# Recurrence heads taken in pairs, scores as 32x32 blocks, and three more query blocks split in high and low parts

## The reference, cut to what matters

```python
q, f_pre, i_v, g, a, a_gate = split(x @ w_in)          # 4 heads of 128 each; a, a_gate: 512 channels
f = lb + (1 - lb) * sigmoid(f_pre)
k = (1 - lb) * sigmoid(-f_pre)
b = cumsum(log(f)) within chunks of 32 tokens          # 8 chunks
q_t = q * exp(b);  k_t = k * exp(-b);  k_end = k * exp(b_last - b)
scores = where(causal, q_t @ k_t.T, 0)                 # 32 x 32 in each chunk and head
o_intra = scores @ v
d_state = k_end.T @ v                                  # 128 x 128 in each chunk and head
state[n + 1] = exp(b_last[n]) * state[n] + d_state[n]
o = o_intra + q_t @ state[n]                           # then rms norm per head, times silu(g)
u = causal_conv31(a * sigmoid(a_gate)) + cv_b          # 31 taps, then layer norm and silu
y = concat(o, u) @ w_out
```

## Time and profile before

| what | before |
|---|---|
| median of 3 runs | 1241.21 us (1241.1 to 1242.23) |
| profiled execution | 1241.21 us |
| its span | 1239.4 us |
| PE, DVE, ACT busy | 1231.4, 801.4, 672.7 us |
| POOL busy | 30.8 us |

### The profile page before, as it was taken

How to read it: one execution, slowest core, us unless ns; L and a number is a source line. 1 busy time by engine, 2 the same in 40 slices (tenths; PEclk the granted TensorE clock), 3 DMA queues, 4 the chain that set the end, 5 groups by cost and what they waited for, 6 DMA issues and landing times. The chain is left out here.

```text
span 1239.4 us, 16273 instructions
## 1 busy us (share of the span) xinstructions
PE 1231.4 (99%) x6332; PEld 1048.4 (85%) x6332; DVE 801.4 (65%) x1185; ACT 672.7 (54%) x1034; POOL 30.8 (2%) x36
## 2 busy tenths in 40 slices
PE   9999999999999999999999999999999999999997
PEld 8888888888888888899988888888888888888886
DVE  5655556878767555568999765755557674755455
ACT  7555546668574444465776745544445754744441
POOL 0000000010000000000001000000001000000000
PEclk9999999999999999999999999999999999999999
DMA  9755556452355555554354632755554443565540
GB/s 368 276 185 178 190 180 201 156 194 85 109 181 187 187 187 187 187 159 174 114 182 158 215 121 104 271 187 188 188 188 166 171 153 119 204 221 189 187 167 34
DMA packets 60891, 219.96 MB, mean 177 GB/s; under 512 B 6672, under 2 KB 8208, under 8 KB 60176
## 3 DMA queue, kind: packets, MB, share of 16 engines
q1 hardware_dynamic: 60528, 218.55, 51.8%
q10 hardware_dynamic: 288, 0.39, 0.1%
HBM read 217.86 MB, written 1.05 MB: 177 GB/s over the span
## 5 line engine op out<-in xcount | busy, mean ns | idle before, releaser
L1212 DVE TENSOR_TENSOR w_lo<-w_raw,w_hi 128x1024 fp32r<-128x1024 f32 x387 | 472.7, 1228 | 341.0 <-ACT w_hi L642 339.9
L642 ACT ACTIVATE w_hi<-w_raw 128x1024 fp32r<-128x1024 f32 x387 | 407.3, 1058 | 421.5 <-PE bank L2049 400.3
L2047 PE MATMUL bank<-w_hi,x_hl 128*128 128x512 f32 (+2 forms) x912 | 357.9, 392 | 0.1
L2049 PE MATMUL bank<-w_hi,x_hl 128*128 128x512 f32 (+2 forms) x912 | 353.1, 387 | 0.0
L2048 PE MATMUL bank<-w_lo,x_hl 128*128 128x512 f32 (+2 forms) x912 | 352.8, 387 | 0.0
L2049 PEld LDWEIGHTS bank<-w_hi,x_hl 128*128 128x128 f32 x912 | 171.2, 188 | 34.9
L2047 PEld LDWEIGHTS bank<-w_hi,x_hl 128*128 128x128 f32 x912 | 171.4, 188 | 34.3 <-issue 0.6
L2048 PEld LDWEIGHTS bank<-w_lo,x_hl 128*128 128x128 f32 x912 | 171.5, 188 | 32.8
L2047 PE MATMUL bank<-w_hi,h_hi 128*128 128x512 f32 (+1 forms) x364 | 141.9, 390 | 0.0
L2049 PE MATMUL bank<-w_hi,h_lo 128*128 128x512 f32 (+1 forms) x364 | 141.3, 388 | 0.0
L2048 PE MATMUL bank<-w_lo,h_hi 128*128 128x512 f32 (+1 forms) x364 | 141.2, 388 | 0.0
(11 more groups left out here) (323 smaller groups left out, 1399.6 us busy)
## 6 DMA issues: line engine op xcount, KB each, us to landing
w_raw<-weights_d SPq DMA_DIRECT2D x394, 512.0 KB, 3.3
arena<-ln_rows_d SPq DMA_DIRECT2D x3, 1024.0 KB, 5.6
arena<-weights_d SPq DMA_DIRECT2D x4, 512.0 KB, 5.0
arena<-late_d SPq DMA_DIRECT2D x1, 1056.0 KB, 8.4
arena<-first_d SPq DMA_DIRECT2D x2, 512.0 KB, 5.5
xs<-x_d SPq DMA_DIRECT2D x2, 512.0 KB, 7.2
kv_mem<-mem_d SPq DMA_DIRECT2D x1, 1024.0 KB, 12.3
out_d<-kv_mem SPq DMA_DIRECT2D x3, 256.0 KB, 2.1
```

The lines of the kernel that those rows point to most:

```text
L642: nc.scalar.activation(w_hi[:, slot(b), :], w_raw[:, b % RAW, :], ACT.Copy).then_inc(hi_ready, 1)
L1212: nc.vector.tensor_tensor(w_lo[:, slot(b), :], w_raw[:, b % RAW, :], w_hi[:, slot(b), :].bitcast(F32), ALU.subtract).then_inc(lo_ready, 1)
L2047: nc.tensor.matmul(out, wh, xh, start=start, stop=False, skip_group_check=True)
L2049: return nc.tensor.matmul(out, wl, xh, start=False, stop=stop, skip_group_check=True)
```

## The change

WHOLE loses steps 12, 13 and 14 of ab_in, so these three query blocks are split. Fewer convolution taps stand ahead of steps 10 to 12, and ACT's taps are spread anew over the steps. Scores are made as 32x32 blocks, only those on the diagonal, side by side in half a bank, and masked in one instruction; their product with v becomes eight 32x32 products a head in place of two of 128x128. The recurrence takes heads 0 and 1, then 2 and 3: changes of state of two heads lie side by side in the four banks, DVE makes the states of both in turns, and PE has the gate blocks 1 and 2 between the changes of the first pair and the wait for its states. States of heads 2 and 3 have a place of their own.

```diff
@@ -85,7 +85,7 @@
     NB += _count
-WHOLE = [FIRST["ab_in"] + n for n in (0, 1, *range(10, 15))]
+WHOLE = [FIRST["ab_in"] + n for n in (0, 1, 10, 11)]
 
@@ -137,7 +137,7 @@
 NCST = 0
-for _name, _cols in [("rows_all", 158), ("causal", P), ("rope", 4 * ROPE), ("dist", 2 * S), ("spread", 4 * P)]:
+for _name, _cols in [("rows_all", 158), ("causal", HG_CHUNK), ("rope", 4 * ROPE), ("dist", 2 * S), ("spread", 4 * P)]:
     CST[_name] = NCST
@@ -153,7 +153,7 @@
     put("rows_all", w)
-    put("causal", (p[:, None] // HG_CHUNK == p[None, :] // HG_CHUNK) & (p[:, None] <= p[None, :]))
+    put("causal", p[:, None] % HG_CHUNK <= np.arange(HG_CHUNK)[None, :])
     pos = np.arange(S, dtype=np.float32)
@@ -255,7 +255,7 @@
 
-        causal = const("causal", 0, P)
+        causal = const("causal", 0, HG_CHUNK)
 
@@ -332,12 +332,12 @@
         eb, _ = region(s0, HG_HEADS, S)
-        sc, _ = region(s0, 2, 512)
+        sc, _ = region(s0, 2 * HG_HEADS, HG_CHUNK)
         s1 = at
...
         go_on = kv_mem[:, 3, 0:4 * S].rearrange("p (a b) -> p a b", b=S)
-        ho_sq_buf, _ = region(s1, 2, HALF)
         s2 = at
+        ho_sq_buf, _ = region(s2, 2, HALF)
         hk, at = region(at, HG_HEADS, S)
@@ -352,9 +352,17 @@
         state = [xs[:, 4 * k:4 * k + 4, 1, :].rearrange("p c (n v) -> p c n v", v=P) for k in range(2)]
+        late_state, late_end = region(s0 + 2 * HG_HEADS * HG_CHUNK, 2 * (NCHUNK - 1), P)
+        assert late_end <= s2
 
         def state_of(h, n):
-            return state[h % 2][:, n // 2, n % 2, :]
+            if h < 2:
+                return state[h][:, n // 2, n % 2, :]
+            return late_state[:, (h - 2) * (NCHUNK - 1) + n - 1, :]
+
+        def change_of(h, n):
+            at = h % 2 * S + n // 4 * P
+            return PB[n % 4][:, at:at + P]
 
@@ -1051,7 +1059,7 @@
 
-            TAP_AT = {4: [(0, 0), (0, 1), (1, 0), (1, 1)], 5: [(0, 2), (1, 2)], 7: [(0, 3), (1, 3)], 8: [(2, 0), (2, 1)], 10: [(2, 2)], 11: [(2, 3)], 13: [(3, 0)], 14: [(3, 1), (3, 2), (3, 3), (4, 0)], 15: [(4, 1)], 16: [(4, 2), (4, 3)], 17: [(5, 0), (5, 1), (5, 2), (5, 3)], 18: [(6, 0), (6, 1), (6, 2), (6, 3)], 19: [(7, 0), (7, 1), (7, 2)]}
+            TAP_AT = {4: [(0, 0), (0, 1), (1, 0), (1, 1)], 5: [(0, 2), (1, 2)], 7: [(0, 3), (1, 3)], 10: [(2, 0), (2, 1)], 11: [(2, 2), (2, 3)], 13: [(3, 0)], 14: [(3, 1), (3, 2)], 15: [(3, 3)], 16: [(4, 0), (4, 1), (4, 2)], 17: [(4, 3), (5, 0), (5, 1), (5, 2)], 18: [(5, 3), (6, 0), (6, 1), (6, 2)], 19: [(6, 3), (7, 0), (7, 1)]}
             ends = flat(bsum).rearrange("p (g s) -> p g s", s=HG_CHUNK)[:, :, HG_CHUNK - 1:HG_CHUNK]
@@ -1098,28 +1106,28 @@
 
-            make_taps([(7, 3), (8, 0), (8, 1), (8, 2), (8, 3)])
-
-            for h in range(HG_HEADS):
-                if h == HG_HEADS - 2:
-                    act.wait_ge(tap_added, 8)
-                    done(FIRST["ab_g"] + 3)
+            make_taps([(7, 2), (7, 3), (8, 0), (8, 1), (8, 2), (8, 3)])
+
+            def squares(pair):
+                act.wait_ge(ho_ps, pair + 1)
+                for h in (2 * pair, 2 * pair + 1):
                     for t in range(2):
-                        nc.scalar.activation(hg[:, t, :], PB[6 + t][:, :], ACT.Silu).then_inc(g_silu, 1)
-                if h == HG_HEADS - 1:
-                    blk()
-                    blk()
-                    mem_blocks(1, 2, 3)
-                act.wait_ge(ho_ps, h + 1)
-                for t in range(2):
-                    w, k = slice(h * P, (h + 1) * P), 2 * h + t
-                    nc.scalar.activation(ho_sq_buf[:, t, w], PB[4 + t][:, w], ACT.Square, accum_out=ho_ss[:, k:k + 1]).then_inc(ho_sq, 1)
-                make_taps(([], [(9, 0), (9, 1), (9, 2), (9, 3)], [], [])[h])
-                if h == 0:
-                    act.wait_ge(ho_sq, 2)
-                    nc.scalar.activation(ho_sq_buf[:, 0, 0:1], decay[:, 0:1], ACT.Silu)
-                elif h < HG_HEADS - 1:
-                    blk()
+                        w, k = slice(h * P, (h + 1) * P), 2 * h + t
+                        nc.scalar.activation(ho_sq_buf[:, t, w], PB[4 + t][:, w], ACT.Square, accum_out=ho_ss[:, k:k + 1]).then_inc(ho_sq, 1)
+
+            blk()
+            blk()
+            nc.scalar.activation(neg_max[0][:, 0:1], decay[:, 0:1], ACT.Silu)
+            squares(0)
+            act.wait_ge(tap_added, 8)
+            done(FIRST["ab_g"] + 3)
+            for t in range(2):
+                nc.scalar.activation(hg[:, t, :], PB[6 + t][:, :], ACT.Silu).then_inc(g_silu, 1)
+            make_taps([(9, 0), (9, 1), (9, 2), (9, 3)])
+            blk()
+            squares(1)
+            blk()
+            mem_blocks(1, 2, 3)
             mem_blocks(1, 3, 5)
@@ -1888,12 +1896,11 @@
                 dve.wait_ge(hk_ready, 4)
-                for t in range(2):
-                    nc.vector.copy_predicated(sc[:, t, :].rearrange("p (h q) -> p h q", q=P), bc(causal.bitcast(I32), HG_HEADS),
-                                              PB[t][:, :].rearrange("p (h q) -> p h q", q=P)).then_inc(sc_ready, 1)
+                nc.vector.copy_predicated(sc[:, :, :], bc(causal.bitcast(I32), 2 * HG_HEADS),
+                                          half(1, 1).rearrange("p (h q) -> p h q", q=HG_CHUNK)).then_inc(sc_ready, 1)
 
             dve.wait_ge(ones_set, 5)
-            ahead = (0, 0, 2, 1, 3, 0, 0, 0, 3, 0, 10, 6, 8, 0, 1, 4, 0, 0, 0, 2)
+            ahead = (0, 0, 2, 1, 3, 0, 0, 0, 3, 0, 7, 3, 5, 0, 1, 4, 0, 0, 0, 2)
             behind_lo = (0, 0, 3, 0, 3, 0, 14, 0, 0, 0, 0, 0, 0, 0, 0, 0, 0, 0, 0, 0)
             add_ahead = {8: (0, 2), 13: (2, 3), 14: (3, 4), 18: (4, 6)}
@@ -1931,27 +1938,37 @@
             add_taps(6, 7)
-            conv_taps(3)
-
-            for h in range(HG_HEADS):
-
-                if h >= 2:
-                    dve.wait_ge(ho_ps, h - 1)
+            conv_taps(4)
+
+            def states(pair):
+                heads = (2 * pair, 2 * pair + 1)
                 dve.wait_ge(e_ready, 3)
-                dve.wait_ge(ds_ps, (NCHUNK - 1) * (h + 1))
-                mark(nc.vector.tensor_copy(state_of(h, 1), PB[0][:, 0:P]))
+                dve.wait_ge(ds_ps, (NCHUNK - 1) * (2 * pair + 2))
+                at = {}
+                for h in heads:
+                    mark(nc.vector.tensor_copy(state_of(h, 1), change_of(h, 0)))
+                    at[h] = chain[0]
                 for n in range(1, NCHUNK - 1):
-                    settle()
-                    ins = nc.vector.scalar_tensor_tensor(state_of(h, n + 1), state_of(h, n),
-                                                         decay[:, h * NCHUNK + n:h * NCHUNK + n + 1],
-                                                         PB[n % 4][:, n // 4 * P:n // 4 * P + P], ALU.mult, ALU.add)
-                    if n < NCHUNK - 2:
-                        mark(ins)
-                ins.then_inc(st_ready, 1)
-                if h >= 2:
-                    blk()
-                add_taps(*((7, 8), (8, 9), (9, 10), (0, 0))[h])
-                conv_taps((2, 2, 0, 1)[h])
+                    for h in heads:
+                        dve.wait_ge(vec_chain, at[h])
+                        ins = nc.vector.scalar_tensor_tensor(state_of(h, n + 1), state_of(h, n),
+                                                             decay[:, h * NCHUNK + n:h * NCHUNK + n + 1],
+                                                             change_of(h, n), ALU.mult, ALU.add)
+                        if n < NCHUNK - 2:
+                            mark(ins)
+                            at[h] = chain[0]
+                        else:
+                            ins.then_inc(st_ready, 1)
+
+            states(0)
+            add_taps(7, 8)
+            conv_taps(4)
+            states(1)
+            add_taps(8, 9)
+            blk()
+            blk()
+            conv_taps(6)
+            add_taps(9, 10)
             blk()
@@ -2691,9 +2708,12 @@
             for t in range(2):
-                s = slice(t * P, (t + 1) * P)
                 for h in range(HG_HEADS):
-                    ins = nc.tensor.matmul(PB[t][:, h * P:(h + 1) * P], kt[:, h, s], hq[:, h, s], start=True, stop=True)
+                    for j in range(4):
+                        r, q = slice(j * HG_CHUNK, (j + 1) * HG_CHUNK), t * HG_HEADS + h
+                        s = slice(t * P + j * HG_CHUNK, t * P + (j + 1) * HG_CHUNK)
+                        ins = nc.tensor.matmul(half(1, 1)[r, q * HG_CHUNK:(q + 1) * HG_CHUNK], kt[:, h, s], hq[:, h, s],
+                                               start=True, stop=True, skip_group_check=True)
             ins.then_inc(sc_ps, 1)
@@ -2716,36 +2736,43 @@
 
+            def changes(pair):
+                for h in (2 * pair, 2 * pair + 1):
+                    for n in range(NCHUNK - 1):
+                        if h == 0 and n == 1:
+                            pe.wait_ge(sc_ready, 1)
+                        r, t = slice(n % 4 * HG_CHUNK, (n % 4 + 1) * HG_CHUNK), n // 4
```

(57 more changed lines are left out.)

## The result

The kernel after the change takes **1248.68 us** (median of 6 runs, 1248.16 to 1249.84), the kernel before 1241.15 us (6 runs, 1240.83 to 1242.23) beside it. The ratio is 1.0062 (1.0051 to 1.0072): slower by 7.5 us. The prediction was 1246.7 us and slower, range 1244.5 to 1252.0. The direction and the range hold. The number is 2.0 us low, and what happened is the forecast and rival 1 together, for which the prediction gave 1249.1 us.

A forecast was written before the change was run, and what follows sets the result against it. DVE, whose last convolution tap PE waits for, was taken to bound the stage. Its first half adds 5.3 us (a 5.0 us wait included), its second 0.2: 1241.2 + 5.5 = 1246.7 us, range 1244.5 to 1252.0.

The forecast's parts named there:

- rival 1: The clock falls in PE's 4.7 us hole ahead of the first gate block, 2.4 us more: 1249.1 us; chance 0.2.
- DVE ends the stage: At the convolution's transposes PE waits for DVE's last tap (0.2 us before), so PE's gains are waited away, DVE's losses kept.
- The missed tap: In step 14 DVE's addition of tap 3 waits for ACT's sixteenth tap, now in step 15: 618.8 to 623.8, +5.0 us.
- Rival 3: The tap in step 14 isn't missed, so no new wait: 1241.9 us, no change; chance 0.07.
- The first half: DVE up to tap 3's addition: nine taps fewer -3.57, three conversions +3.41, scan +0.4; with the wait and 0.1, +5.3 us.
- the second half: DVE from there to the last tap: masks -0.9, states -2.9, nine late taps +3.6, waits for PE +0.4: +0.2 us.
- States and masks: DVE's head work: paired state steps 0.26 us apart for 0.384, -2.9 us; one mask copy of about 0.36 us, -0.9 us.
- PE's own work: PE in this stage: about 2.0 us less, 1.7 from three split blocks and some 0.3 net from head work.
- the scores: On PE, 64 small score instructions at 28 ns take 1.8 us, no change; bounds 1.3 and 7.2 us.
- PE's holes: New PE waits: 1.5 us ahead of the transposes of k, 4.7 us ahead of the first gate block.
- Rival 2: The 32x32 masked products in one bank don't overlap, 1.3 us more a head: about 1251.7 us; chance 0.12.
- Rival 4: DVE doesn't end the stage, its last tap comes before PE, so PE's savings show: 1238.0 us; chance 0.04.

The follow-up runs named there:

- e2: The changed kernel with 27 unused products of ones with ones filling PE's two holes, all waits kept: 1246.17 us, ratio 1.004.
- e3: The changed kernel with the three query blocks whole again and the tap lists of before, head work still in pairs: 1239.84 us, ratio 0.9989 against before.
- e1: The changed kernel with ACT making tap (3, 3) in step 14 again, not in step 15: 1242.86 us, ratio 1.001 against before.
- e4: The kernel before with the three query blocks split and the changed tap lists, tap (3, 3) in step 14, heads one by one: 1245.77 us, ratio 1.0038.
- e8: The changed kernel with DVE adding tap 3 in step 16 in place of step 14, ACT's taps unchanged: 1243.9 us, ratio 1.0022 against before.
- e7: The changed kernel with tap (3, 3) back in step 14 and 8 unused products ahead of the first gate block: 1241.52 us, ratio 1.0002 against before.

## Why the prediction was right, and where its terms were off

The forecast was made for full clock, 1246.7 us. e2, in which the clock stays up and the wait is left, took 1246.17. So the mechanism and its size were right, and the 2.0 us by which the number is low are the term that the forecast left out: the low clock (+2.5), less 0.5.

**DVE ends the stage: right.** In after the transposes of the convolution wait for DVE's last tap, and the shift of that tap is the shift of the end. e3 shows the other side: as soon as DVE is 3.9 us early, PE is next, after 1.3 us.

**The missed tap, +5.0 us: right, 4.9 us.** The count of 16 and ACT's place of (3, 3) at 623.8 were as worked out (623.84 to 624.34). The addition starts 5.37 us after the tap ahead of it (619.00 to 624.37), in e1 0.61 us, so the wait adds 4.8 us. e1 shows that this entry is the cause, and e2 that the 4.8 us reach the end.

**The balance without the wait: right.** Rival 3 gave 1241.9 us for the change with no missed tap; e1's undisturbed runs took 1241.4. The first half came to +0.06 us at the addition in e1 (forecast +0.3: the scan starts 0.2 us later in e1, at 612.64 for 612.41, where the sum has 0.4), the second half to 0.0 (forecast +0.2). The prediction isn't of one piece here: its own scan times, 612.7 for 612.41, differ by 0.3, and it puts the addition at 618.8 "as in before" while its sum has it 0.3 us later. So three conversions for three blocks is a bad trade where DVE ends the stage, and the head work in pairs just pays for it. e4 and e3 show the two parts by themselves at +4.6 us (some of it the clock) and -1.3 us.

**States and masks: right.** 0.26 us a step as forecast, 0.33 us for the mask (0.36). Together 3.6 to 3.9 us by e4 and e3, forecast 3.8.

**The range: too wide below.** Its lower end, 1244.5 us, is said to be the wait 1 us shorter and the states at their best, 0.6 us more. That is 1.6 us off 1246.7, or 1245.1. The measured time lies in the upper half, where rival 1 is.

**PE's own work: -2.0 us, and its sum is off.** Its own prices give 1.7 us for the blocks and 4 x 0.2 = 0.8 us for the masked products, 2.5 us and not 2.0. In e1 the scores start 1.80 us sooner than in before (629.99 for 631.79), which is the blocks as priced; the scores then save another 1.1 us, and the masked products 0.3 us in place of 0.8. None of it reaches the time: PE waits 2.34 us for the v copies and 1.06 us for the last tap.

**PE's holes: right in place, 2.5 and 4.5 us for 1.5 and 4.7.** The first is longer mainly for one reason, the scores. **That term was mis-sized.** I priced 64 instructions at 28 ns each, 1.8 us, with a lower bound of 1.3 us, whose 20 ns came from no row. They took 0.76 us: (0.76 - 0.20)/63 = 9 ns apart. By itself this changed nothing at the end of the stage, since PE waits for DVE right behind them; it made the hole 1 us longer. Whether the clock would also have fallen with a first hole of 1.5 us, as forecast, no run shows.

**The clock: the step of the sum that failed.** The forecast left it at full speed, and gave the fall 0.2. It fell in all six runs (mean clock 0.995, 0.999 before). The price was right: 2.4 us forecast, 2.5 measured by e2. What I misread is when. I measured the 4.7 us hole against the 4.8 us of idleness at the kernel's end, and named the first hole without counting with it. The clock fell near 635.2, when the second hole, from 635.14, had only begun. What stood before the fall was the first hole of 2.5 us and 1.1 us of transposes; the second hole can only have kept the clock low. e8 shows the same with a hole of 3.2 us behind the transposes (its gate block begins at full speed at 634.94, and the mean of 0.67 over 634 to 638 puts the fall 0.4 us later), and e4 with one of 3.1 us. So the end of the kernel was too mild a yardstick, and the chance should have been well over 0.2. The Trainium skill ("TensorE: Matmul & The Clock Gate", "HAM oscillation") warns of idle gaps that drop the clock, and the trace agrees that they do. The holes come from the wait of the forecast itself, so forecast and rival were no alternatives: the second follows from the first. The prediction named the low clock behind the hole as a sign of being wrong, and this sign came.

**Rival 2, no overlap of 32x32 products in one bank: wrong.** The 16 masked products of a head take 0.64 us, (0.64 - 0.27)/15 = 25 ns apart (28 in the forecast), with four row groups writing four partition ranges of one bank. By the Trainium skill ("TensorEngine Tiling (Array Packing)", "Gotcha 1: PSUM Pressure") different row tiles can't access one bank at once; here they do no worse than with a bank each, 35 ns, and the measurement decides. My reason for 0.12, that the rule may be meant for tiles sharing columns, is in line with it, but no run here tests tiles that share columns. The gain was smaller than priced all the same: from a head's first masked product to its first state product it is 0.57 us in e1 (644.91 to 645.48), for 0.64 in before and 0.45 in the forecast.

**Rival 4, faster: wrong.** The path that it describes exists, though: in e3, which has no wait of 5.0 us and no split blocks, DVE comes out 3.9 us early and the kernel is faster, by 1.3 us.

What stays open: whether after's first hole alone would always drop the clock. e2 fills both, and no run of after fills one and leaves the other at its length.

## What to carry to other kernels

When an instruction is moved past a counted semaphore's wait, count again what the n-th signal now is and what stands ahead of it in that engine's program; here one list entry cost 4.8 us, and 2.5 us more by the clock. Idle time of TensorE has a second price, the clock: holes of 2.3 to 3.2 us let it fall here, in some executions or in nearly all, and what follows a hole then runs at half the clock for a while (3.4 us behind e4's). And before work is moved from the busiest engine (three blocks, 1.7 us of PE) to another (3.4 us of DVE), look at which of them ends the stage and which of its results the first one waits for in the middle.

## What the runs showed that I had not expected

- The 64 score instructions (fp32, stationary 128x32, 32 columns) are 9 ns apart in the profile, for 112 ns between the 128x128 ones that they replace, and 28 ns of other 128x32 ones with 128 columns.
- A single hole of 2.3 us in e1 goes with a lower mean clock in six of eleven executions, and not in the other five: about 1243 and 1241.4 us from one program. A fill of 8 products removes the split (e7). A kernel with such a hole has two times, and its median says which happened more often.
- The clock came back late in after: dense work began at 639.6 and the clock was full only at 645.4. All of its cost (2.5 us) lies behind the holes, in the gate block. After e4's hole of 3.1 us it fell only when the matmuls had begun again.
